# A mixture-of-experts kernel: expert lists made ahead of the loop, and results added on DVE instead of by an accumulating scatter

## The reference, cut to what matters

```python
scores = sigmoid(t @ w_router); ...            # 64 experts, groups, top 8 of them per token
gates  = sum(one_hot(top_e, 64) * w_sel[..., None], axis=1)
def expert_step(acc, xs):                      # for each of the 64 experts
    wg, wu, wd, g = xs
    h = silu(t @ wg) * (t @ wu)                # (1024 x 256) twice
    return acc + (h @ wd) * g[:, None], None   # (256 x 1024)
shared = (silu(t @ w_gate_s) * (t @ w_up_s)) @ w_down_s
x = LN(ALPHA * x + routed + shared)
```

## Time and profile before

| | us |
|---|---|
| median of three runs | 1381.57 |
| the profiled execution | 1380.71 |
| its span, first to last instruction | 1378.9 |
| span up to the first matmul of expert 0 | 612.4 |
| first matmul of expert 0 to the last of expert 63 | 728.5 |
| from there to the end | 38.0 |

### The profile page before, as it was taken

One profiled execution on the slowest core, in us unless ns is written; L12 is line 12 of the kernel. 1 busy time (PEld: TensorE's weight loads), 2 busy tenths in 40 slices (PEclk: granted clock), 3 DMA queues, 4 the chain that ended last, 5 costly groups with the idle time before them and its releaser, 6 DMA issues.

```text
span 1378.9 us, 18465 instructions
## 1 busy us (share of the span) xinstructions
PE 1238.7 (90%) x6931; PEld 973.4 (71%) x6931; DVE 776.1 (56%) x1095; ACT 543.3 (39%) x722; POOL 407.6 (30%) x385
## 2 busy tenths in 40 slices
PE   6899878899999899969999999999999999999980
PEld 6899756799999896336666666666666666666750
DVE  3123596431333545257776666666666677777745
ACT  3232475422122211125544444444444444445522
POOL 2000343201110114343433343333444433433223
PEclk9999898699999997989999999999999999999995
DMA  9671301023224119148999999999999999999954
GB/s 296 175 133 33 102 1 69 1 65 99 82 77 161 67 59 403 50 145 291 360 357 339 347 343 345 339 345 346 344 348 346 340 340 338 342 344 349 354 101 154
DMA packets 91617, 314.75 MB, mean 228 GB/s; under 512 B 15698, under 2 KB 48644, under 8 KB 66324
## 3 DMA queue, kind: packets, MB, share of 16 engines
q1 hardware_dynamic: 65616, 257.03, 48.3%
q0 software_dynamic: 18688, 53.37, 18.9%
q10 hardware_dynamic: 7252, 3.50, 1.8%
HBM read 284.30 MB, written 45.22 MB: 239 GB/s over the span
## 4 chain that ended last, share of the span: by engine, by line
PE 71%; DVE 10%; DMA 7%; issue 5%; ACT 2%; POOL 2%; ACTq 2%; DVEq 0%; POOLq 0%
PE bank L1929 23%; PE bank L1949 13%; PE bank L1665 9%; PE bank L1666 9%; DMA y_rows<-ysb,idx_u 6%; PE bank L1824 4%; DVE onehot L1505 3%; PE bank L1680 3%; PE bank L1892 3%; PE bank L1854 2%; ACTq L877 2%; DVE L L1260 1%; DVE mx L1266 1%; PE bank L1871 1%; PE bank L1845 1%
## 5 line engine op out<-in xcount | busy, mean ns | idle before, releaser
L1529 DVE TENSOR_TENSOR wgu_lo<-wgu,wgu_hi 128x4096 fp32r<-128x4096 f32 x64 | 282.7, 4418 | 3.1 <-ACT wgu_hi L1129 3.0
L789 POOL TENSOR_TENSOR spare<-spare 128x1 f32<-128x1 f32 x128 | 120.3, 940 | 448.6 <-DMA y_rows<-ysb,idx_u 409.2
L1949 PE MATMUL bank<-wd,hT 128*128 128x512 f32 x512 | 230.1, 592 | 0.9 <-DVE hT L1539 0.9
L1129 ACT ACTIVATE wgu_hi<-wgu 128x4096 fp32r<-128x4096 f32 x63 | 227.4, 3610 | 0.9 <-DMA wgu<-in_w_up_e_dram 0.9
L1929 PE MATMUL bank<-wgu_hi,xgT 128*128 128x512 f32 x512 | 206.2, 403 | 2.4
L1929 PE MATMUL bank<-wgu_hi,xgT_lo 128*128 128x512 f32 x512 | 200.8, 392 | 0.0
L1929 PE MATMUL bank<-wgu_lo,xgT 128*128 128x512 f32 x512 | 200.6, 392 | 0.0
L1133 ACT ACTIVATE silu<-bank 128x256 f32<-128x256 f32 x64 | 24.6, 384 | 368.9 <-PE bank L1929 368.9
L1949 PEld LDWEIGHTS bank<-wd,hT 128*128 128x128 f32 x512 | 96.7, 189 | 98.0 <-issue 92.0
L1545 DVE COPY ysb<-bank 128x512 f32<-128x512 f32 x64 | 44.3, 692 | 163.1 <-PE bank L1949 160.6
L1929 PEld LDWEIGHTS bank<-wgu_hi,xgT 128*128 128x128 f32 x512 | 96.7, 189 | 23.3 <-issue 0.5
(11 more groups left out here) (287 smaller groups left out, 2431.7 us busy)
## 6 DMA issues: line engine op xcount, KB each, us to landing
wgu<-in_w_gate_e_dram SPq DMA_DIRECT2D x64, 1024.0 KB, 9.2
wgu<-in_w_up_e_dram SPq DMA_DIRECT2D x64, 1024.0 KB, 13.6
wd<-in_w_down_e_dram SPq DMA_DIRECT2D x64, 1024.0 KB, 7.7
raw<-in_w_in_dram SPq DMA_DIRECT2D x16, 1024.0 KB, 6.2
raw<-in_w_proj_a_dram SPq DMA_DIRECT2D x4, 1024.0 KB, 5.2
raw<-in_w_out_dram SPq DMA_DIRECT2D x4, 1024.0 KB, 5.2
x_lo_kept<-xT_lo SPq DMA_DIRECT2D x1, 2304.0 KB, 11.6
x_lo_back<-x_lo_kept SPq DMA_DIRECT2D x1, 2304.0 KB, 8.2
```

Of the source, the lines that this page charges most:

```text
L789: pool.tensor_tensor(spare[:, i:i + 1], spare[:, 0:1], spare[:, 0:1], ALU.mult).then_inc(s, 1)
L1129: act.activation(wgu_hi[u % 2][:], wgu[u % WSLOTS][:], ACT.Copy).then_inc(hi_by_act, 1)
L1529: v.tensor_tensor(wgu_lo[u % WSLOTS][:], w_[:], wgu_hi[u % 2][:].bitcast(F32), ALU.subtract).then_inc(lo_by_dve, 1)
L1949: last = mm(bank[3 + h][:, :], hT[:, u % 2, j, :], wd[slot][:, j, h * 512:(h + 1) * 512], start=j == 0, stop=j == FE // P - 1)
```

## The change

The lists are made once, ahead of the loop. DVE makes for each token and each of its 8 experts a slot number (position times 64 plus expert, slot_u; the largest 8 of a row by MAX8). POOL writes each token's number to that slot of a table in HBM (owner) with 40 indirect DMAs of one 4-byte element per partition, waits for all of them, and reads the first 128 positions of all experts back in one DMA (idx_all). The gates ride along as 64 more columns of x1_rows, so a gathered row brings its gates. R, the one-hot rows and PE's list products are gone, and so is POOL's tiny instruction in the loop; places() moves forward to t == 1.

The result is no longer added by DMA. There are three accumulators in HBM (y_rows 0 to 2, NACC = 3; experts take turns, the last four use two of them). For each expert POOL gathers the accumulator's rows (gather_y), DVE adds both halves from PSUM to them (y_add), and POOL scatters them back plainly. Unused places are skipped on both ways. In each step POOL waits for DVE's weight split (lo_by_dve), then issues gather_y two experts ahead of y_add, then the token gather, then the scatter. ACT takes over ht_evac, DVE the whole of the result, the shared expert's product and its sum with ALPHA times x1. All 64 steps are written out; no hardware loop is left. Behind the loop three accumulators are read back, and DVE adds them per tile. POOL clears two accumulators with 10 DMAs during the attention; SP fills the owner table with skipped indices with 5 DMAs near the start.

```diff
-    x1_rows = nc.dram_tensor("x1_rows", (TOK, D), F32, kind="Internal").ap()
-    y_rows = nc.dram_tensor("y_rows", (TOK + P, D), F32, kind="Internal").ap()
+    DG = D + E
+    x1_rows = nc.dram_tensor("x1_rows", (TOK, DG), F32, kind="Internal").ap()
+    y_rows = [nc.dram_tensor(f"y_rows{i}", (TOK, D), F32, kind="Internal").ap() for i in range(NACC)]
+    owner = nc.dram_tensor("owner", (NT * P * E, 1), U32, kind="Internal").ap()
...
@@ POOL
+            pool.wait_ge(owner_cleared, 16 * NT)
+            pool.wait_ge(route_dve, 1)
+            for t, (a, w) in enumerate(TILES):
+                for r in range(8):
+                    pool.indirect_dma_start(out=owner, out_offset=bass.IndirectOffsetOnAxis(slot_u[0:w, t, r:r + 1], 0),
+                                            in_=token_id[0:w, t:t + 1], in_offset=None).then_inc(owner_written, 16)
+            pool.wait_ge(owner_written, 16 * NT * 8)
+            pool.dma_start(idx_all[:, :], owner.rearrange("(t p e) a -> t p (e a)", t=NT, p=P)[0]).then_inc(idx_landed, 16)
...
+            def next_y(e):
+                pool.wait_ge(y_put[acc[e]], 16 * (turn[e] - 1))
+                gather_y(acc[e], idx_all[:, e:e + 1])
+            for e in range(E):
+                if e + 2 < E:
+                    pool.wait_ge(lo_by_dve, e + 2)
+                n = e if e >= E - 2 else e + NACC - 2
+                if NACC <= n and (n < E - 2 or n == e):
+                    next_y(n)
+                if e + XGSLOTS < E:
+                    pool.wait_ge(h_by_dve, e + 1)
+                    pool.wait_ge(ex_xt, e + 1)
+                    gather_x(e % XGSLOTS, xg_in[e % XGSLOTS], idx_all[:, e + XGSLOTS:e + XGSLOTS + 1])
                 if e >= 1:
-                    scatter(e - 1, e - 1, e == 1)
+                    pool.wait_ge(y_by_dve, 2 * e)
+                    scatter_y(acc[e - 1], idx_all[:, e - 1:e])
...
@@ DVE
-            def y_evac(e, u, free=True):
+            def y_add(e, i):
                 v.wait_ge(ex_dn, e + 1)
-                if free:
-                    v.wait_ge(y_added, (e - 1) * 16)
-                v.tensor_copy(ysb[:, u % 2, 512:1024], bank[4][:, :]).then_inc(y_by_dve, 1)
+                for h in range(2):
+                    c = slice(h * 512, (h + 1) * 512)
+                    v.tensor_tensor(yg[i][:, c], yg[i][:, c], bank[3 + h][:, :], ALU.add).then_inc(y_by_dve, 1)
...
+            for e in range(E):
+                if e + 1 < E:
+                    xt_evac(e + 1, e + 1)
+                    weights_lo(e + 1, e + 1)
+                hidden(e, e, slice(D + e, D + e + 1))
+                if e >= 1:
+                    v.wait_ge(y_got[acc[e - 1]], 16 * turn[e - 1])
+                    y_add(e - 1, acc[e - 1])
...
@@ PE
+            for e in range(E):
+                if e + 1 < E:
+                    rows_t(e + 1, e + 1, 16 * ((e + 1) // XGSLOTS + 1))
+                gate_up(e, e)
+                if e >= 1:
+                    down(e - 1, e - 1, (e - 1) // WSLOTS + 1)
+                hidden_t(e, e)
...
@@ behind the loop, DVE
+                v.wait_ge(y_back[t], 32)
+                then(v.tensor_tensor(x1[0:w, t, :], x1[0:w, t, :], y_other[0][0:w, t, :], ALU.add))
+                if NACC > 2:
+                    v.wait_ge(y_third, 16 * NT)
+                    then(v.tensor_tensor(x1[0:w, t, :], x1[0:w, t, :], y_other[1][0:w, t, :], ALU.add))
```

More of the change, by code:

```diff
@@ L22 @@
 BUCKET_FAR = 128
-UNROLL = 8
 WSLOTS = 4
@@ L267, in hybrid_layer @@
     y_at = h0 + wslot_bytes
-    ysb = place("ysb", [P, 2, D], F32, y_at)
+    yg_at = [y_at, y_at + D * 4, j0 + JBYTES - D * 4]
+    yg = [place(f"yg{i}", [P, D], F32, yg_at[i]) for i in range(NACC)]
+    assert j_at[0] <= yg_at[2]
+    acc = [e % NACC if e < E - 4 else e % 2 for e in range(E)]
+    turn = [acc[:e + 1].count(acc[e]) for e in range(E)]
+    uses = [acc.count(i) for i in range(NACC)]
     assert y_at + 2 * D * 4 <= h0 + RAW * DC * SB * 4
@@ L665, in _ @@
             sp.wait_ge(most_dve, 1)
             sp.wait_ge(ex_dn, E)
+            for i in range(NACC):
+                sp.wait_ge(y_put[i], 16 * uses[i])
             most_r = sp.value_load(most[0:1, 0:1], min_val=0, max_val=TOK)
             with sp.If(most_r > P):
+                if NACC > 2:
+                    sp.wait_ge(y_third, 16 * NT)
                 for tile in range(1, NT):
+                    if tile > 1:
+                        sp.wait_ge(y_put[0], 16 * (uses[0] + E * (tile - 1)))
+                    sp.dma_start(idx_all[:, :], rows[tile]).then_inc(idx_again, 16)
@@ L833, in _ @@
+            for e in range(XGSLOTS):
+                gather_x(e, xg_in[e], idx_all[:, e:e + 1])
             pool.wait_ge(y_inited[0], 16 * ((NT + 1) // 2))
             pool.wait_ge(y_inited[1], 16 * (NT // 2))
[L835 to L843 removed]
@@ L1170, in _ @@
+            ex_ht_evac(E - 1, E - 1)
+            for i in range(NACC):
+                act.wait_ge(y_put[i], 16 * uses[i])
             most_r = act.value_load(most[0:1, 0:1], min_val=0, max_val=TOK)
@@ L1559, in _ @@
-            v.wait_ge(sy_dve, 1)
-            v.wait_ge(pool_sy, NT - 1)
-            xt_evac(0, 0)
-            v.wait_ge(y_inited[0], 16 * ((NT + 1) // 2))
-            v.wait_ge(y_inited[1], 16 * (NT // 2))
-            def step(e, u, first=False, ahead=True, wait=True, last=False, free=True):
-                if ahead:
-                    hot(e + IDX_AHEAD, u + IDX_AHEAD)
-                if not first:
-                    ht_evac(e - 1, u - 1)
-                if not last:
-                    weights_lo(e + 1, u + 1)
-                    xt_evac(e + 1, u + 1)
-                if ahead:
-                    idx(e + IDX_AHEAD, (u + IDX_AHEAD) % UNROLL, wait)
-                hidden(e, u)
-                if not first:
-                    y_evac(e - 1, u - 1, free)
@@ L1579, in _ @@
-            for e in range(UNROLL):
-                step(e, e, first=e == 0, wait=e + IDX_AHEAD >= UNROLL, free=e >= 3)
-            with v.Fori(1, E // UNROLL - 1) as i:
-                for u in range(UNROLL):
-                    step(i * UNROLL + u, u)
-            for e in range(E - UNROLL, E):
-                step(e, e % UNROLL, ahead=e + IDX_AHEAD < E, last=e == E - 1)
-            ht_evac(E - 1, E - 1)
-            y_evac(E - 1, E - 1)
-            v.wait_ge(y_added, 16 * E)
+            sh_sum(4)
@@ L1590, in _ @@
+            for i in range(NACC):
+                v.wait_ge(y_put[i], 16 * uses[i])
             most_r = v.value_load(most[0:1, 0:1], min_val=0, max_val=TOK)
@@ L1924, in gate_up @@
                 pe.wait_ge(lo_by_dve, e + 1)
-                if wait:
+                if not (isinstance(e, int) and e == 0):
                     pe.wait_ge(h_by_dve, e)
```

473 lines of the change are left out of this document (191 added, 282 removed).

## The result

The changed kernel takes 1538.43 us (median of four runs, 1524.9 to 1557.6; the slowest run is left out of the ratio), the kernel before 1381.37 beside it: a ratio of 1.111, 95% interval 1.103 to 1.118. The prediction was 1325, range 1305 to 1365, with 0.85 on faster. It is wrong in sign.

The account below looks back on a forecast made before the run. Two close limits bound the loop, PE's list and DMA. Loop -75, ahead +6, elsewhere +1, behind +12 sum to -56 on the profiled span, giving 1325 us; range 1305 to 1365, 0.85 on faster.

Parts of the forecast that it names:

- PE's floor: Loop: PE's step without list work is 10.03 us; 10.15 was taken, making the loop 75 us shorter.
- POOL's new waits: Loop: gather_y waits for POOL's scatter just before; the round, 7.1 to 12.1 us, was put at 9.5, hidden under 10.15.
- A lead of 17 us: Loop: both gathers are issued two to three steps ahead, so about 17 us of lateness can build up before PE notices.
- rival D: Loop: POOL's round takes the accumulating scatter's landing, 12.1 us; +123, 1448 us; chance 0.05.
- DMA per step: Loop: weights plus three small transfers need 9.2 to 11.5 us of DMA time per step, likely 9.9 to 10.3.
- Rival A: Loop: DMA or POOL's round sets the step at about 10.6 us; +28, 1353 us; chance 0.20.
- Rival C: Loop: bytes per second limit DMA, a step takes 11.6 us; +91, 1416 us, slower; chance 0.08.
- The split: Ahead of the loop: half of a weight split's 4.42 us counted as delaying POOL's issues; by the skill's rule, 2.2 us less.
- Ahead of the loop: Before the first gate_up: 40 owner-list issues at 1.06 us, landing, read-back and gather; +6 us.
- Rival B: Ahead of the loop: each owner-list issue costs as much as the accumulating scatter's, 1.58 us; +21, 1346 us; chance 0.15.
- Behind the loop: After the last matmul: more reads and DVE additions, some held by POOL's bias additions; +12 us, from +7 to +18.

Follow-up runs that it names:

- e1: The changed kernel without the scatters except the last on each accumulator, so routed contributions are not summed up: 1321.97 us.
- e13: e9 with the down weights not loaded but for a small corner from the fifth expert on; instructions, waits and issues stay: 1320.19 us.
- e2: The changed kernel with gather_y issued one POOL round later, so it waits for the scatter of one round earlier: 1411.78 us.
- e3: The changed kernel with DVE's weight split over an eighth of the tile from the second expert on: 1468.58 us.
- e9: e2 with the places spread over both halves of the partitions, place j on partition 64 (j mod 2) + j div 2: 1383.85 us.
- e10: The changed kernel without the y gather, its scatter accumulating on three accumulators, places spread over both halves of the partitions: 1377.0 us.
- the first spread: e2 with list place j read back to partition 8 (j mod 16) + j div 16 instead of partition j: 1403.91 us.
- e8: The changed kernel without POOL's wait for DVE's weight split at the head of its step: 1482.08 us.

## Why the prediction was wrong

*What bounds the kernel, PE's floor.* Right: 10.03 us was read from the last steps, e1 and e13 run at 9.99 and 9.98. With that step the sum would have been 1315; their 1322 and 1320 us are that and about the 7 us by which the end behind the loop was missed.

*POOL's new waits: the step that failed.* The prediction named the chain (landing, gather_y, token gather, next scatter), made its round 9.5 us and called it hidden. It is 13.6. Term by term: the landing was 7.1 and is 7.7 in the mean (median 7.5, 4.2 to 12.3). The two issues behind it were 2 x 1.05 and are 2.02 + 2.38 = 4.4, since in 39 of 41 rounds one issue is held by the weight split. The hold had a row and was priced ahead of the loop, but not in the round. Waking was 0.3 and is 0.8, and the gaps between issues, which had no term, are (14.2 + 12.5) / 41 = 0.65. That makes 13.6. The landing came out near its price by luck: it was measured at a DMA share of 0.79, while the prediction had the share near 1, and in e2 at 0.91 a scatter takes 17.9 us. So pricing the holds would not have saved the step; in e3, without them, the round is still longer than 12 us. A lead of 17 us was held against this. A lead covers lateness once; a round that is 3.5 us longer than the step eats it in some five steps. The prediction said so ("a longer round sets the step, one for one"), and the round's own upper bound, 12.1, was above 10.15. It stood in rival D with 0.05. With a bound of 7.1 to 12.1 against 10.15, that chance was far too low, and the 12.1 itself left out the holds.

*What is late next.* Missed as well: PE, once it waits for tokens, loses half of its clock for some us (0.50 from 964 to 970 us), so the lateness costs more than itself.

*DMA per step: low.* The forecast was 9.9 to 10.3. In e9, with all engines at work, weights take 73.9% of 550 us over some 48.7 steps (11.3 us each in that window), 8.35 us instead of 7.6; POOL's queue takes 21.5%, 2.43 or 0.81 for each of three transfers, within the 0.75 to 0.9 taken. That is 10.8 us at a share of 0.96: 11.2 a step, if DMA time alone sets it. So the likely end of "9.2 to 11.5" was the wrong one, for the weights' price beside small rows (a packet of 8 KB takes 344 ns in the mean of e9's records, 322 in before's). Rival A's mechanism (DMA sets the step) fits e9 and e10, at a higher price. Rows on 9 of 16 engines, T2, came up nowhere in the prediction; before doesn't show it, since its scatter writes all 128 rows.

*Rival C* came near e2's step and time (11.6 and 1416, measured 11.33 and 1412) for the wrong reason: bytes per second. e9 moves more GB/s than e2 with the same bytes per step (362 against 352), and e1 ran at 371. The Trainium skill (DMA: Bandwidth & Descriptors, Specifications) gives an HBM limit of about 358 GB/s per core, as half of a stack's 716. The 371 GB/s of e1 over 550 us are above it; this program runs on one core.

*The split.* Issues of 1.0 us that met a split took 4.08, 3.67 and 5.17 us, and in e3 a small split leaves them at 1.0 to 1.2 in the mean. The Trainium skill (SBUF — State Buffer, Who interferes with whom) infers that a subtraction of two SBUF tiles does not hold descriptor generation; these rows disagree with the inference.

*Ahead of the loop.* Right in the sum, in part by luck: +6.8 for a predicted +7, with 40 issues of 0.97 and gaps of 0.30, 1.27 each against 1.06 (+8 us), most of it made up by a start at 549.0 instead of 555.3. One issue took 4.41 us, a hold of 3.4 where 3.6 was allowed. Rival B (1.58 per issue) is out.

*Behind the loop.* +18.8 against +12 and just outside +7 to +18: the addition of the third accumulator takes 3.24 us instead of 1.2 in three tiles (the holds were foreseen at about 1 each, they are 2), and the first addition starts 10.8 us behind the last scatter's issue, where some 9 was allowed.

## What to carry to other kernels

Where an engine's list holds a wait for its own last DMA, that round is a step of its own: add landing and all issues behind it, each at its price beside the neighbour that can hold it, and compare the sum with the step, for no lead covers a round that is longer. Then ask how old the transfer waited for is: one round more took back 127 of the 157 us here (1538 to 1412). A buffer that is gathered, changed and scattered is a loop as well: add both landings and the work between, divide by the number of buffers, and compare that with the step too. And count rows per DMA engine, not per queue: a high mean share can hide that half of the engines are idle for part of the time.

## What the runs showed of the hardware

- An indirect DMA's issue on POOL, 1.0 us alone, takes up to 5.17 us when it meets a 4.42 us DVE subtraction of two SBUF tiles; in the changed kernel all 56 held issues of the loop end 0.88 to 0.91 us behind that subtraction.
- An indirect DMA's rows are dealt to the DMA engines by their partition. 66 rows on partitions 0 to 65 run as eight chains of eight and one of two; in the first spread, on partitions p with p mod 8 under 4 and on 4 and 12, as eight of eight and two of one; taken half from partitions 0 to 32 and half from 64 upward, 16 at a time. All three fit an engine for each pair of (p div 64, (p div 4) mod 8); this is inferred from the three patterns.
- The landing of the same kind of scatter took 7.5 us at the median in the changed kernel (DMA share 0.79), 9.8 in e13 (0.88) and 17.9 in e2 (0.91).
- Between a landing and the issue that waits for it lie 0.74 us in the changed kernel, and 0.26 in e8, which has one wait less in front of the issue.
- Skipped places are not free of packets: the last scatter has 78 packets of 4 bytes, 7 to 9 ns each, for 62 skipped places and 16 engines.
- POOL leaves 0.30 us between two such issues that wait for nothing.
- Behind the loop, DVE additions of 1.22 us took 3.24 in three tiles beside a POOL addition, and POOL's own took 3.25, where it took 2.33 in the kernel before.
- Still open: why a weight packet takes longer beside small rows (309 ns at the median in all runs, the mean 322 in before, 331 to 344 in the others and 362 in e13), and how much of the last 0.8 to 1.1 us a step of e10 and e9 over PE's floor is DMA time alone.
